# Expert rows fetched and added one stage later, a layer norm's scale and offset applied after the transposes, and a weight split moved into the expert stage

## The reference

```python
h = layer_norm(DEEPNORM_ALPHA * h + mix, ln_mix_g[layer], ln_mix_b[layer])
ffn = hier_moe(h, ...)     # 16 experts of width 256, two chosen for each row
h = layer_norm(DEEPNORM_ALPHA * h + ffn, ln_ffn_g[layer], ln_ffn_b[layer])
```

## Time and profile before

| what | us |
|---|---|
| runs | 2655.59, 2656.32, 2656.4 (median 2656.32) |
| profiled execution, its own time | 2657.57 |
| its span | 2655.7 |
| PE busy | 2418.2 (91%) |
| DVE busy | 1212.0 (46%) |
| ACT busy | 1030.3 (39%) |
| POOL busy | 828.7 (31%) |

### The profile page before, as it was taken

How to read it: one execution, slowest core, us unless ns; L and a number is a source line. 1 busy time by engine, 2 the same in 40 slices (tenths; PEclk the granted TensorE clock), 3 DMA queues, 4 the chain that set the end, 5 groups by cost and what they waited for, 6 DMA issues and landing times. The chain is left out here.

```text
span 2655.7 us, 34098 instructions
## 1 busy us (share of the span) xinstructions
PE 2418.2 (91%) x13040; PEld 1895.4 (71%) x13040; DVE 1212.0 (46%) x2393; ACT 1030.3 (39%) x1738; POOL 828.7 (31%) x281
## 2 busy tenths in 40 slices
PE   6999999879977989997996699999999899999998
PEld 5888888667745866576774567667887757677886
DVE  3555542455435347846453544363122354362123
ACT  4444342134532147724553324543223424543222
POOL 2442442324442320022334222324442322324442
PEclk9999998879987989997998799999999999999999
DMA  5126111158864231115887321313322421314311
GB/s 134 48 57 230 40 48 64 54 189 284 280 232 136 85 127 50 36 50 189 281 284 238 104 87 48 107 57 121 119 92 74 131 63 53 100 64 159 96 64 72
DMA packets 251564, 315.20 MB, mean 119 GB/s; under 512 B 52608, under 2 KB 168656, under 8 KB 251424
## 3 DMA queue, kind: packets, MB, share of 16 engines
q1 hardware_dynamic: 249120, 304.89, 35.9%
q0 software_dynamic: 2304, 8.39, 0.8%
HBM read 277.46 MB, written 35.79 MB: 118 GB/s over the span
## 5 line engine op out<-in xcount | busy, mean ns | idle before, releaser
L159 POOL TENSOR_TENSOR branch_weights_wl<-branch_weights_wf,branch_weights_wh 128x2048 fp32r<-128x2048 f32 (+1 forms) x66 | 302.1, 4577 | 728.9 <-ACT branch_weights_wh L153 728.9
L153 ACT ACTIVATE branch_weights_wh<-branch_weights_wf 128x2048 fp32r<-128x2048 f32 (+1 forms) x66 | 124.7, 1889 | 209.3 <-PE merge_acc L201 93.4
L201 PE MATMUL bmid_acc<-xh,branch_weights_wh 128*128 128x512 f32 x320 | 148.9, 465 | 8.9 <-PEq L72 8.9
L201 PE MATMUL merge_acc<-xh,branch_weights_wh 128*128 128x512 f32 x384 | 151.5, 395 | 3.4 <-PEq L72 3.4
L538 POOL TENSOR_TENSOR in_weights_wl<-in_weights_wf,in_weights_wh 128x1024 fp32r<-128x1024 f32 x32 | 79.4, 2481 | 237.2 <-ACT in_weights_wh L534 219.7
L201 PE MATMUL merge_acc<-xh,branch_weights_wl 128*128 128x512 f32 x384 | 151.4, 394 | 0.0
L201 PE MATMUL merge_acc<-xl,branch_weights_wh 128*128 128x512 f32 x384 | 151.4, 394 | 0.0
L159 POOL TENSOR_TENSOR nsa_weights_wl<-nsa_weights_wf,nsa_weights_wh 128x2048 fp32r<-128x2048 f32 x13 | 60.3, 4643 | 289.2 <-ACT nsa_weights_wh L153 289.2
L201 PE MATMUL bmid_acc<-xl,branch_weights_wh 128*128 128x512 f32 x320 | 127.4, 398 | 0.0
L201 PE MATMUL bmid_acc<-xh,branch_weights_wl 128*128 128x512 f32 x320 | 127.3, 398 | 0.0
L1636 POOL TENSOR_TENSOR rt_wl<-rt_wf,rt_wh 128x2048 fp32r<-128x2048 f32 x16 | 82.6, 5160 | 127.8 <-ACT rt_wh L1632 127.8
(11 more groups left out here) (609 smaller groups left out, 6525.3 us busy)
## 6 DMA issues: line engine op xcount, KB each, us to landing
branch_weights_wf<-w_in SPq DMA_DIRECT2D x56, 1024.0 KB, 5.1
rt_wf<-moe_w_down SPq DMA_DIRECT2D x32, 1024.0 KB, 5.6
in_weights_wf<-gdn_w_in SPq DMA_DIRECT2D x64, 256.0 KB, 3.4
rt_wf<-moe_w_gate SPq DMA_DIRECT2D x32, 512.0 KB, 7.3
rt_wf<-moe_w_up SPq DMA_DIRECT2D x32, 512.0 KB, 8.1
moe_rows<-rt_y SPq DMA_DIRECT2D x64, 256.0 KB, 2.1
moe_rows<-gdn_z SPq DMA_DIRECT2D x2, 6144.0 KB, 27.7
merge_bwf<-w_branch SPq DMA_DIRECT2D x12, 1024.0 KB, 5.0
```

Source lines behind the costliest of these rows:

```text
L153: act.activation(self.h[u][:, :, 0:self.cols(b)], self.s.f[u][:, :, 0:self.cols(b)], ACT.Copy).then_inc(self.s.hi_ready, 1)
L159: pool.tensor_tensor(self.l[u][:, :, 0:self.cols(b)], self.s.f[u][:, :, 0:self.cols(b)], self.h[u][:, :, 0:self.cols(b)].bitcast(F32), ALU ...
L201: mm = pe.matmul(self.acc[:, s, 0:cols], lhs[:, P * s:P * s + P], rhs, start=(u == 0 and k == 0 and n == 0), stop=(u == 1 and k == HALF - ...
```

## The change

1. In both layers POOL's 8 gathers and DVE's 8 adds leave the expert stage (class `RowsBack`) and stand at the start of the next stage: POOL starts the gathers first thing, DVE adds tile t just before its statistics. In the NSA stage they land in the room of `qt` and `kt`, which is not yet used.
2. After layer 0 the norm is `LateNorm`. DVE computes only (h - mean) * inv (`normal`). PE turns this. In the turned tile a column is a partition, so ACT applies scale and offset as per-partition operands while it reads PSUM, 4 instructions of 128x128 for each half, and then copies to `xh`. `xl` is taken from the ACT result in SBUF. The full h is still needed later, so DVE multiplies and adds the vectors (`finish`, two tensor_tensor for each tile, 8 in all) between and after the copies of block V's accumulators. Two small loads bring the vectors as [partition, k].
3. `hi_second` and `lo_second`: unit 1 of the next stage's first block is split at the end of the expert stage, in both layers.

```diff
+    def hi_second(self, act):
+        self.hi(act, 0, 1)
+
+    def lo_second(self, pool):
+        self.lo(pool, 0, (1,))
...
+    def gather(self, pool):
+        for t in range(TT):
+            for k in range(2):
+                pool.indirect_dma_start(self.tiles[t][:, k, :], None, self.g.moe_rows[:, :],
+                                        bass.IndirectOffsetOnAxis(self.left.slot_i[:, k, t:t + 1], 0)).then_inc(self.back[t], 16)
+
+    def add(self, dve, t):
+        h = self.g.h[:, t, :]
+        dve.wait_ge(self.back[t], 32)
+        for k in range(2):
+            if k:
+                dve.wait_ge(self.added, 2 * t + 1)
+            dve.scalar_tensor_tensor(h, self.tiles[t][:, k, :], self.left.weight[:, k, t:t + 1], h,
+                                     ALU.mult, ALU.add).then_inc(self.added, 1)
+        dve.wait_ge(self.added, 2 * t + 2)
...
+    def normal(self, dve, t):
+        h = self.g.h[:, t, :]
+        dve.wait_ge(self.rooted, t + 1)
+        dve.reciprocal(self.inv[:, t:t + 1], self.dev[:, t:t + 1]).then_inc(self.inverted, 1)
+        dve.wait_ge(self.inverted, t + 1)
+        dve.tensor_scalar(h, h, self.mv[:, t, 0:1], self.inv[:, t:t + 1], ALU.subtract, ALU.mult).then_inc(self.done, 1)
...
+    def turn(self, pe, t):
+        pe.wait_ge(self.done, t + 1)
+        for half in range(2):
+            if t >= 2:
+                pe.wait_ge(self.spread, 2 * t + half - 3)
...
+    def hi(self, act, t):
+        for half in range(2):
+            n = 2 * t + half
+            act.wait_ge(self.turned, n + 1)
+            if n >= 2:
+                act.wait_ge(self.lo_done, n - 1)
+            for k in range(HALF):
+                col = HALF * half + k
+                ins = act.activation(self.rooms[half][:, k, :], self.bank(t, half)[:, k, :], ACT.Identity,
+                                     scale=self.left.gain[:, col:col + 1], bias=self.left.shift[:, col:col + 1])
+            ins.then_inc(self.spread, 1)
+            act.wait_ge(self.spread, n + 1)
+            act.activation(self.place(self.g.xh, t, half), self.rooms[half], ACT.Copy).then_inc(self.hi_done, 1)
+
+    def lo(self, dve, t):
+        for half in range(2):
+            dve.wait_ge(self.hi_done, 2 * t + half + 1)
+            dve.tensor_tensor(self.place(self.g.xl, t, half), self.rooms[half],
+                              self.place(self.g.xh, t, half).bitcast(F32), ALU.subtract).then_inc(self.lo_done, 1)
+
+    def finish(self, dve, t, gain, shift):
+        h = self.g.h[:, t, :]
+        dve.wait_ge(self.turned, 2 * t + 2)
+        dve.tensor_tensor(h, h, gain, ALU.mult).then_inc(self.scaled, 1)
+        dve.wait_ge(self.scaled, t + 1)
+        dve.tensor_tensor(h, h, shift, ALU.add).then_inc(self.finished, 1)
...
                 def stats(t):
+                    rows.add(dve, t)
...
                     load_vector(sp, 1, "ln_ffn_b")
+                    for x, name in ((rt.left.gain, "ln_ffn_g"), (rt.left.shift, "ln_ffn_b")):
+                        sp.dma_start(x[:], a[name][layer].rearrange("(k p) -> p k", p=P),
+                                     allow_slow_non_contiguous=True).then_inc(ln_in, 16)
...
                     act.activation(ht[:].rearrange("p k n -> p (k n)"), ps_t[:, 0, 0:HID], ACT.Copy).then_inc(ht_out, 1)
+                    if last:
+                        act.wait_ge(gu_done, i)
+                        nxt.hi_second(act)
...
                 nxt.lo_first(pool)
-                pool.wait_ge(added, 1)
-                for t in range(TT):
-                    for k in range(2):
-                        pool.indirect_dma_start(rows_back[t][:, k, :], None, rows[:, :],
-                                                bass.IndirectOffsetOnAxis(rt.slot_i[:, k, t:t + 1], 0)).then_inc(back[t], 16)
...
                 end = pairs(dve, body, scale)
                 for c in range(2):
                     dve.wait_ge(y_stored[c], end * 32 + 32)
-                dve.tensor_copy(slot[:, 0, 0:1], slot[:, 1, 0:1]).then_inc(added, 1)
-                dve.wait_ge(scaled, 1)
-                for t in range(TT):
-                    dve.wait_ge(back[t], 32)
-                    for k in range(2):
-                        if k:
-                            dve.wait_ge(scaled, 2 + t)
-                        ins = dve.scalar_tensor_tensor(g.h[:, t, :], rows_back[t][:, k, :], rt.weight[:, k, t:t + 1],
-                                                       g.h[:, t, :], ALU.mult, ALU.add)
-                        if not k:
-                            ins.then_inc(scaled, 1)
+                dve.tensor_copy(slot[:, 0, 0:1], slot[:, 1, 0:1])
...
-                sp.wait_ge(norm.done, TT)
+                sp.wait_ge(norm.finished, TT)
...
                 for t in range(TT):
-                    pe.wait_ge(norm.done, t + 1)
-                    turn.pe(pe, t)
+                    norm.turn(pe, t)
                     if t:
-                        pe.wait_ge(turn.lo_done, 2 * t)
+                        pe.wait_ge(norm.lo_done, 2 * t)
                         ws.multiply_tile(pe, t - 1, g.xh, g.xl)
-                pe.wait_ge(turn.lo_done, 2 * TT)
+                pe.wait_ge(norm.lo_done, 2 * TT)
                 ws.multiply_tile(pe, TT - 1, g.xh, g.xl)
                 narrow.multiply(pe)
...
-                ws.lo(pool, 0, (1,))
+                rows.gather(pool)
                 compress.clear(pool)
...
-                ws.hi(act, 0, 1)
                 for t in range(TT):
                     norm.root(act, t)
                     if t:
-                        turn.hi(act, t - 1)
-                turn.hi(act, TT - 1)
+                        norm.hi(act, t - 1)
+                norm.hi(act, TT - 1)
...
-                def stats(t):
-                    for half in range(2):
-                        norm.stats(dve, t, half)
-
                 link = Link(dve, step)
-                stats(0)
-                for t in range(TT):
-                    norm.centre(dve, t, 2 * t + 2)
-                    norm.finish(dve, t)
-                    if t + 1 < TT:
-                        stats(t + 1)
-                    if t == 0:
-                        narrow.split(dve, 16)
-                    if t:
-                        turn.lo(dve, t - 1)
-                turn.lo(dve, TT - 1)
-                for t in range(TT):
+
+                def take(t):
                     dve.wait_ge(ws.acc_ready, t + 1)
                     dve.tensor_copy(n.v[:, t, :], ws.acc[:, t, :]).then_inc(ws.evicted, 1)
+
+                narrow.split(dve, 16)
+                rows.add(dve, 0)
+                norm.stats(dve, 0)
+                for t in range(TT):
+                    norm.normal(dve, t)
+                    if t + 1 < TT:
+                        rows.add(dve, t + 1)
+                        norm.stats(dve, t + 1)
+                    if t:
+                        norm.lo(dve, t - 1)
+                norm.lo(dve, TT - 1)
+                for t in range(TT - 1):
+                    take(t)
+                for t in range(2):
+                    norm.finish(dve, t, n.vec[:, 0:D], n.vec[:, D:])
+                take(TT - 1)
+                for t in range(2, TT):
+                    norm.finish(dve, t, n.vec[:, 0:D], n.vec[:, D:])
                 narrow.copy(dve)
...
-                ws.lo(pool, 0, (1,))
+                if layer:
+                    ws.lo(pool, 0, (1,))
...
```

More of the change, by code:

```diff
@@ L1237, in finish, with __init__ @@
         dve.scalar_tensor_tensor(h, h, self.inv[:, t:t + 1], self.shift[:], ALU.mult, ALU.add).then_inc(self.done, 1)
+class RowsBack:
+    def __init__(self, g, st, left, tiles):
+        self.g, self.left, self.tiles = g, left, tiles
+        self.back, self.added = [st.sem(f"rows_back{t}") for t in range(TT)], st.sem("rows_added")
+    def gather(self, pool):
[12 more added lines that the diff above has]
+        dve.wait_ge(self.added, 2 * t + 2)
@@ L1425, in _, with stage_ffn_norm @@
                 logits.take(dve, g.logits)
-def stage_ffn_norm(g, name, vectors, pre_gain):
+def stage_ffn_norm(g, name, rt, pre_gain):
     nc = g.nc
     with Stage(nc, name) as st:
-        norm = LayerNorm(g, st, None, None, vectors)
+        ws = rt.weights
+        rows = RowsBack(g, st, rt.left, [x[:].rearrange("p (k a) n -> p k (a n)", k=2) for x in (ws.f[0][2], *ws.f[1])])
+        norm = LayerNorm(g, st, None, None, rt.vectors)
         pre = PreNorm(g, st, pre_gain) if pre_gain else None
@@ L1440, in _ @@
                     pre.load(sp)
+            @block.gpsimd
+            def _(pool):
+                rows.gather(pool)
             @block.tensor
@@ L1662, in stage_experts @@
         y_out, y_stored = ([st.sem(f"{x}{c}") for c in range(2)] for x in ("y_out", "y_stored"))
-        back = [st.sem(f"back{t}") for t in range(TT)]
         ln_in = st.sem("ln_loaded")
-        scaled, added = st.sem("scaled"), st.sem("added")
```

(13 more changed lines are left out.)

51 lines of the change are left out of this document (41 added, 10 removed).

## The result

The changed kernel takes 2665.62 us (median of 20 executions, 2658.08 to 2669.12), the kernel before 2656.57 beside it (20 executions). The ratio is 1.0032, 95% interval 1.0026 to 1.0038: slower by 8.5 us, 6.9 to 10.1. Forecast were 2658.2 and a range of 2649.5 to 2664.0. The profiled execution took 2669.03, 11.5 over the one of before (2657.57). It is the second longest of its twenty, 3.4 above their median, so some 3 of the 11.5 are the choice of the execution and not the change.

The account below looks back on a forecast made before the run. PE, busy 91% of the span, was taken to bound the kernel. Layer 0's -0.3 (-9.5 + 7.3 + 1.9) and layer 1's +2.2 gave +1.9 on the median 2656.32: 2658.2 us, range 2649.5 to 2664.

Parts of the forecast that it names:

- The layer 0 start: From layer 0's expert end to block V: NSA stage starts 18.2 us earlier, block V's first product 9.5 earlier.
- Rivals 3 and 4: Layer 0: gathers starve beside RAW weights, 2662.8, chance 0.15; moved split ends the expert stage late, 2660.1, chance 0.07.
- The layer 0 tail: Around the first gate matmul: gates' turn waits for DVE's copy, a stall of 7.3 us plus 1.9 of lower clock.
- rival 1: Layer 0's tail: DVE and POOL run side by side, gate copy is in time, 2649.0 us; chance 0.10.
- rival 2: Layer 0's tail: POOL's unit 1 waits for DVE's last four operations, stall 2.7, 2651.7 us; chance 0.08.
- Layer 1: Layer 1's expert end to norm: the stage now ends only when the second norm vector lands, +2.2 us.
- Other edits at no cost: The two small vector loads and SP's waits before bias rows and Q0's last weights: nobody waits, no cost.

Follow-up runs that it names:

- layer 1 alone: The kernel before with only layer 1's part of the change, layer 0 as before: 2659.10 us, ratio 1.0009 to the kernel before.
- `layer0_only`: The changed kernel with layer 1's gathers, adds and splits put back into the old stages: 2663.60 us, ratio 1.0022 to the kernel before.

## Why the prediction was wrong

**The layer 0 start: right.** The stage started 1.55 behind the small copy (forecast 1.6), the moved split ended at 782.60, before DVE at 782.87 (0.3 of cover, forecast 0.2). Block V started 8.4 earlier and not 9.5: POOL began its gathers 0.8 behind the other engines, and the first add came 8.55 behind the first gather (I took 7.9 for the two together). From then on DVE waited for no rows. Rivals 3 and 4 are out.

**The layer 0 tail: right.** The first four operations began 4.6 ahead of the first gate matmul, as forecast, at 1.22 each and not 1.3. POOL's two splits began 0.5 ahead of it and ended 10.3 behind it (forecast 11.1), and DVE's fifth and sixth operation waited for them, one each. The turn came 14.4 behind the first gate matmul (forecast 15.8), with PE idle for 5.89 (7.3), released by DVE's copy. At the turn the changed kernel was 2.2 ahead of the one before (67.61 behind the small copy, 69.81 before), at RAW's first copy 0.06 behind it: the clock cost 2.3, forecast 1.9. DVE and POOL excluded each other for whole instructions, as the Trainium skill's rule on the shared ports has it (SBUF — State Buffer, section "SBUF: two separate sides"): 5.07 and 5.47 for 1.22. Together +0.1, forecast -0.3. That the sum is so near is in part luck: the start won 1.1 less than forecast, the stall cost 1.4 less. Rivals 1 and 2 are out.

**Layer 1: right, a little low.** The next stage started 5.8 behind the small copy (forecast 5.5), the first add came 7.6 later (7.0), and the adds hid 1.2 (1.2). That would be +3.3; the branch projection's first copy then came 13.35 behind its stage's start and not 13.92, at a mean granted clock of 0.86 for 0.82, which was luck. To that copy it is +2.7, and the runs of layer 1 alone give +2.4 (0 to 4.5); forecast +2.2.

**What failed is the step "Other edits at no cost".** It costed loads and waits, and not that new tiles move all those behind them. The placement alone costs 2.7 us (0.3 to 5.0), 2.4 of which the two expert stages show. With layer 1's 2.4 and layer 0's 0.1 that is 5.2 of the 8.5. The forecast had +1.9, so this term is 2.7 of the 6.6 that it missed, the sizes of the others 0.6, and with it alone the forecast would have been 2660.9.

**The rest, about 3 us, is not settled.** The times alone don't even show that it is there: with the intervals of the three measurements (1.6, 2.4 and 2.3 either side) the 3.3 is uncertain by an estimated 3.7, and with the medians' 4.5 for the placement it is half as large. The granted clock over the whole span was 0.9503 in the mean of the 20 executions of the changed kernel and 0.9513 in that of the 99 of the kernel before that ran beside the experiments, not beside it. At half clock instead of full that is 0.0010 x 2 x 2660 = 5.3 us of time and some 2.7 us of work. But not all of it is time lost: by the two profiles 1.8 of the 2.7 lie between layer 1's small copy and the projection (0.57 over 67.85 us for 0.58 over 65.17), where PE mostly waits and the cost is counted already. `layer0_only`, whose layer 1 is as before, had 0.9506 against 0.9514 in the same runs, which is 2 us; single executions of one kernel differ by 0.001 as well. So the clock may be 1 or 2 of the 3. The profiles show where such time can lie, in stretches that nobody edited, and that one of them varies by up to 6.2 us with the same instructions. Whether the changed kernel gets more of it than the kernel before, and why, was not shown. I had put such a loss, 1.9, only right behind the stall, and had no rival for the rest of the span. (A slip in the chances: rival 1 and half of rival 2 make 0.14, not 0.16.)

## What to carry to other kernels

Cost the allocations of a change as well as its instructions: compare the tiles' addresses of both versions, and if they moved, time the old kernel with the new placement; spare bytes that put the tiles back at the same place modulo 256 gave back the experts' stretches here. Ask of a small copy that PE waits for what stands ahead of it on its engine, and move what nobody waits for behind it (8.4 us here, for one line moved). A wait that is taken off one transfer by starting it beside another can return as the other's delay: of 2.9 us won in layer 1, 2.0 came back. And ask what the end of a stage waits for before you start transfers in it for the next one: four gathers started early held it for 5 us. Last, don't explain a difference of a few us in an unedited stretch from one profile each.
